# First modulation rows made in column strips beside the first norm, and the second norm's rows made between its tiles

## What is computed

```python
mod = jax.nn.silu(c) @ w_ada[l] + b_ada[l]            # [1, 6*1024]; w_ada is 1024 x 6144, f32
sh_m, sc_m, gt_m, sh_f, sc_f, gt_f = jnp.split(mod, 6, axis=-1)
h = modulate(rmsnorm(x, g_norm_mix[l]), sh_m, sc_m)    # h * (1 + sc) + sh
z = h @ w_in[l]                                        # r, k, v and low-rank columns, latent attention columns, gates
... RWKV-7 time mixing, latent attention ...
x = x + gt_m * ((sigmoid(gates) * branches) @ w_out)
h = modulate(rmsnorm(x, g_norm_ffn[l]), sh_f, sc_f)
x = x + gt_f * hierarchical_moe(h)
```

## Time and profile before

| | before |
|---|---|
| median of 3 runs | 1671.89 us (1671.5 to 1673.9) |
| profiled execution, its own time | 1669.98 us |
| its span | 1668.2 us |
| PE busy | 1427.4 us, 86% of the span |
| DVE busy | 704.3 us, 42% |
| ACT busy | 464.2 us, 28% |
| POOL busy | 249.0 us, 15% |
| mean granted TensorE clock | 0.923 of full |
| HBM read and written | 211.00 MB and 44.58 MB |

### The profile page before, as it was taken

One profiled execution on the slowest core, in us unless ns is written; L12 is line 12 of the kernel. 1 busy time (PEld: TensorE's weight loads), 2 busy tenths in 40 slices (PEclk: granted clock), 3 DMA queues, 4 the chain that ended last, 5 costly groups with the idle time before them and its releaser, 6 DMA issues. The chain is left out here.

```text
span 1668.2 us, 32819 instructions
## 1 busy us (share of the span) xinstructions
PE 1427.4 (86%) x14321; PEld 1024.3 (61%) x14321; DVE 704.3 (42%) x991; ACT 464.2 (28%) x827; POOL 249.0 (15%) x292
## 2 busy tenths in 40 slices
PE   7499999847999984499988999999896699999980
PEld 3497777627999981277767888787785333333320
DVE  1545677566666636144444111355335221111114
ACT  0543223252434322144434222212111111111110
POOL 0001122105656520011110000000000100000003
PEclk9699999978999997699998999999997699999995
DMA  6711222100000009990002111314106789999957
GB/s 256 251 56 51 83 81 83 58 15 2 5 4 4 4 8 318 313 371 1 1 1 76 50 50 50 139 51 152 42 39 260 265 326 420 421 421 401 410 212 302
DMA packets 76582, 252.35 MB, mean 151 GB/s; under 512 B 7128, under 2 KB 32216, under 8 KB 59680
## 3 DMA queue, kind: packets, MB, share of 16 engines
q1 hardware_dynamic: 66800, 220.48, 35.4%
q0 software_dynamic: 6048, 16.79, 2.8%
q10 hardware_dynamic: 3600, 13.11, 1.9%
HBM read 211.00 MB, written 44.58 MB: 153 GB/s over the span
## 5 line engine op out<-in xcount | busy, mean ns | idle before, releaser
L2418 PE MATMUL ps<-gu,xT 128*32 128x512 f32 x1536 | 178.3, 606 | 4.6 <-DMA gu<-w_e_up 3.9
L394 PE MATMUL ps<-hs,wh 128*128 128x512 f32 x320 | 126.7, 396 | 11.5 <-DVE hs L390 7.9
L396 PE MATMUL ps<-hs,wl 128*128 128x512 f32 x320 | 126.5, 395 | 0.0
L2418 PEld LDWEIGHTS ps<-gu,xT 128*32 128x32 f32 x1536 | 48.2, 112 | 111.6 <-issue 107.6
L2640 DVE TENSOR_TENSOR sg<-sg,ps 128x256 f32<-128x256 f32 x25 | 10.5, 422 | 217.3 <-ACT sg L2504 217.3
L395 PE MATMUL ps<-hs,wh 128*128 128x512 f32 x256 | 100.6, 393 | 0.0
L390 DVE TENSOR_TENSOR wl<-wraw,wh 128x1024 fp32r<-128x1024 f32 x24 | 29.4, 1225 | 156.2 <-ACT wh L387 156.2
L394 PE MATMUL ps<-hh,wr_h 128*128 128x512 f32 x224 | 93.1, 416 | 0.6 <-DVE wr_l L390 0.6
L395 PE MATMUL ps<-hl,wr_h 128*128 128x512 f32 x224 | 88.4, 395 | 0.0
L396 PE MATMUL ps<-hh,wr_l 128*128 128x512 f32 x224 | 88.4, 395 | 0.0
L1895 DVE TENSOR_REDUCE nmax<-ps 128x1 f32<-128x896 f32 (+4 forms) x64 | 45.9, 754 | 99.9 <-PE ps L1804 99.4
(11 more groups left out here) (358 smaller groups left out, 3037.0 us busy)
## 6 DMA issues: line engine op xcount, KB each, us to landing
gu<-w_e_gate SPq DMA_DIRECT2D x34, 1024.0 KB, 13.8
gu<-w_e_up SPq DMA_DIRECT2D x34, 1024.0 KB, 16.3
dn<-w_e_down SPq DMA_DIRECT2D x34, 1024.0 KB, 12.6
wada<-w_ada SPq DMA_DIRECT2D x16, 1024.0 KB, 6.7
expert_rows<-YTM ACTq DMA_DIRECT2D x25, 512.0 KB, 8.8
wbuf<-w_ada SPq DMA_DIRECT2D x4, 2048.0 KB, 15.5
wraw<-w_gates SPq DMA_DIRECT2D x16, 512.0 KB, 3.4
expert_rows<-zrow SPq DMA_DIRECT2D x4, 2048.0 KB, 24.6
```

The costliest lines, as they stand in the source:

```text
L394: nc.tensor.matmul(out, wt[0], mov[0], start=(k == 0), stop=False)
L396: return nc.tensor.matmul(out, wt[1], mov[0], start=False, stop=(k == kn - 1))
L2418: last = nc.tensor.matmul(ps[part, GB[b]], xT[:, b, k, part], gu[:, expert(m, c_) % WB, :, k], start=(k == 0), stop=(k == KD - 1))
```

## The change

Phase 0 is gone. Rows 0 and 1 are made at the start of phase 1 by `rows0`, with the strips of `Rows`: 8 pieces of 1 MB, each with its own slot. The result lies in four strips of one tile; four matmuls with a selection matrix `sel` as weights copy each strip to 128 partitions in PSUM, and ACT and DVE copy it to `SH_M` and `SC_M`. `rows4` moves from phase 4 into phase 1: 16 pieces of 256 columns (0.5 MB) with 3 slots, two pieces on PE after the transposes of each tile. The subtraction that gives `wm_l` moves from DVE to GpSimd. In phase 4 only `rows2` is left, with 6 slots, one piece per tile; pair 0 is loaded ahead of it, pairs 1 to 3 behind it and ahead of the stores of the results.

```diff
 class Rows:
-            def __init__(self, st, col, bank, row, other=None):
+            def __init__(self, st, col, bank, row, wbuf, crep, rep_s):
+                self.room, self.width = wbuf.shape[1], wbuf.shape[3]
+                self.pieces = KD * 512 // self.width
...
+            def load(self, sp, i):
+                if i >= self.room:
+                    sp.wait_ge(self.mm, i - self.room + 1)
+                at = slice(i // KD * self.width, (i // KD + 1) * self.width)
+                src = w_ada_v[:, i % KD, self.col:self.col + 2 * D].rearrange("p (j n) -> p j n", j=CH)[:, :, at]
+                sp.dma_start(self.wbuf[:, i % self.room], src).then_inc(self.w_in[i % self.room], 16)
...
-        with phase() as st:
...
-                    for b in range(CH):
-                        pe.wait_ge(w_in_s[b], 16)
-                        for k in range(KD):
-                            m = nc.tensor.matmul(ps[:, b], crep[:, k], wbuf[:, b, k],
-                                                 start=(k == 0), stop=(k == KD - 1))
...
 @block.sync
+                    sp.dma_start(ccol[:], c[0].rearrange("(p k) -> p k", k=KD)).then_inc(c_in, 16)
+                    sp.dma_start(cst[:], consts).then_inc(const_in, 16)
+                    rows0.load_bias(sp)
...
+                    for k in range(KD):
+                        rows0.load(sp, k)
+                        if k % 2:
+                            load_x(k // 2)
+                    sp.dma_start(wm[:], w_mla).then_inc(wm_in, 16)
+                    rows4.load_bias(sp)
...
+                    for i in range(NW):
+                        rows4.load(sp, i)
...
                     for t in range(NT):
+                        if t + 4 < NT:
+                            sp.wait_ge(h_ready, t + 1)
+                            load_x(t + 4)
+                        for i in range(NW + 2 * t, min(NW + 2 * t + 2, rows4.pieces)):
+                            rows4.load(sp, i)
+                        if t:
+                            store(t - 1)
+                    store(NT - 1)
+                    rows4.store(sp, 2)
 @block.gpsimd
+                    pool.wait_ge(wm_hi, 1)
+                    nc.gpsimd.tensor_tensor(wm_l[:], wm[:], wm_h[:].bitcast(f32), ALU.subtract).then_inc(wm_lo, 1)
 @block.scalar
+                    act.wait_ge(bc_mm, 1)
+                    nc.scalar.activation(SH_M, ps[:, 0:2].rearrange("p a n -> p (a n)"), ACT.Copy).then_inc(sh_ev, 1)
 @block.vector
+                    roots(0)
+                    rows0.add_bias(dve, CH + 2)
+                    dve.wait_ge(rows0.done, 1)
+                    nc.vector.scalar_tensor_tensor(row0[64:P], row0[64:P], 1.0, gains[64:P], ALU.add, ALU.mult)\
+                      .then_inc(rows0.done, 1)
+                    dve.wait_ge(bc_mm, 1)
+                    link(nc.vector.tensor_copy(SC_M, ps[:, 2:4].rearrange("p a n -> p (a n)")))
...
-                                low_part(wm_l[:], wm[:], wm_h[:]).then_inc(wm_lo, 1)
...
+                    rows4.add_bias(dve, CH + 2)
 @block.tensor
+                    for k in range(KD):
+                        rows0.products(pe, k)
+                    pe.wait_ge(rows0.done, 2)
+                    for j in range(CH):
+                        m = nc.tensor.matmul(ps[:, j], sel[:, j], row0, start=True, stop=True)
...
+                        for i in range(2 * t, 2 * t + 2):
+                            rows4.products(pe, i)
                         if t >= 2:
                             mla(t - 2)
 # phase 4, sync
+                    pair(0)
                     for k in range(KD):
                         rows2.load(sp, k)
-                    pair(0)
-                    for k in range(KD):
-                        rows4.load(sp, k)
-                    rows2.store(sp, 1)
+                    for p in range(1, HEADS // 2):
+                        pair(p)
                     for half in range(2):
                         sp.wait_ge(fin, NT * (half + 1))
...
-                    rows4.store(sp, 2)
-                    for p in range(1, HEADS // 2):
-                        pair(p)
+                    rows2.store(sp, 1)
 # phase 4, tensor
-                    for i in range(EARLY):
-                        row_products(i)
...
+                        rows2.products(pe, t)
```

More of the change, by code:

```diff
@@ L418, in build @@
             rot = alias("rot", [P, 2, 2, QK, 16], f32)
-            with ExitStack() as scratch:
-                ang = sb(scratch, "ang", [P, NT, 16])
-                turns = sb(scratch, "turns", [P, NT, 16])
+            arows = alias("arows", [P, 3, 512], f32)
+            row0, row4, gains = (arows[:, i] for i in range(3))
             sqk = sb(st, "sqk", [P, QK, QKD])
+            c_in, c_sig, rep_s, const_in, pc_in, sel_s, bc_mm, sh_ev = sems(
+                st, "c_in", "c_sig", "arep", "const_in", "pc_in", "sel_s", "bc_mm", "sh_ev")
+            rows0 = Rows(st, 0, 6, row0, wbuf0, crep, rep_s)
+            rows4 = Rows(st, 4 * D, 7, row4, wbuf4, crep, rep_s)
             x_in = slots(st, "x_in", 4)
@@ new lines, in _ @@
+                    for k in range(KD):
[4 more added lines that the diff above has]
+                    rows4.load_bias(sp)
+                    for j in range(2):
+                        half = slice(j * 512, (j + 1) * 512)
+                        sp.dma_start(gains[QUARTERS[j]], g_norm_ffn[:, half].broadcast_to([32, 512]))\
+                          .then_inc(rows4.b_in, 16)
@@ new lines, in _ @@
+                    for i in range(NW):
+                        rows4.load(sp, i)
+                    for b in range(2):
+                        sp.dma_start(wr[:, b], w_rwkv[b]).then_inc(wr_in[b], 16)
+                    sp.dma_start(pc[:], pcol).then_inc(pc_in, 16)
+                    sp.dma_start(posi[:], pos).then_inc(m_in, 16)
+                    sp.dma_start(g_row[:].rearrange("p a n -> p (a n)"),
+                                 qk_gain.broadcast_to([P, 2 * QKD])).then_inc(m_in, 16)
@@ L650, in tile_low, with roots @@
                         low_part(hl[:, :, cols], stage[:, t % 2], hh[:, :, cols]).then_inc(h_lo, 1)
-                    for half in range(2):
+                    def roots(half):
                         cols = slice(4 * half, 4 * half + 4)
@@ L670, in _ @@
                         tile_low(4 * half + 3)
+                    rows4.add_bias(dve, CH + 2)
+                    dve.wait_ge(rows4.done, 1)
+                    nc.vector.scalar_tensor_tensor(row4[0:64], row4[0:64], 1.0, gains[0:64], ALU.add, ALU.mult)\
+                      .then_inc(rows4.done, 1)
                     for b in range(2):
@@ L1595, in _ @@
                     rows2.load_bias(sp)
-                    rows4.load_bias(sp)
-                    for j in range(2):
-                        sp.dma_start(gffn[QUARTERS[j]], g_norm_ffn[:, j * 512:(j + 1) * 512].broadcast_to([32, 512]))\
-                          .then_inc(rows4.b_in, 16)
                     def pair(p):
```

145 lines of the change are left out of this document (50 added, 95 removed).

## The result

| | before | changed |
|---|---|---|
| median | 1672.33 us (1671.5 to 1673.9, 4 runs) | 1655.19 us (1648.97 to 1657.26, 4 runs) |
| profiled execution, its own time | 1669.98 us | 1648.97 us |
| its span | 1668.2 us | 1647.2 us |

The ratio is 0.989, 95% interval 0.9863 to 0.9918: faster by 17 us, inside the stated range of 1635 to 1657, but 8.7 us short of the forecast of 1646.5, outside the forecast's own 1640 to 1652 and only 1.8 us from the 1657 of rival 2.

The account below looks back on a forecast made before the run. TensorE idles at both changed places: the start, bound by DMA after the change, and the end of phase 4, bound by SP's loads and stores. +2.1 - 27.5 = -25.4 us gives 1644.6 profiled, 1646.5 median; range 1635 to 1657.

Parts of the forecast that it names:

- rival 2: Weights' DMA time was already hidden: stores wait for the drained queue (-19), phase 1 loses 4; 1657 us, chance 0.14.
- The likeliest case: The forecast itself: +2.1 us in phase 1, -27.5 in phase 4, 1646.5 us, own range 1640 to 1652, chance 0.66.
- What bounds the kernel: Both changed places have TensorE idle; strips save 22 us of TensorE time, but DMA takes over and keeps most.
- First scaling: Start of phase 1: first tile starts at 46.2 us instead of 52.88, 6.7 us sooner.
- the stream: Start of phase 1: 10.5 MB at 387 GB/s from 7.5 us, so the fourth tile of x lands at 34.6.
- The subtraction on GpSimd: Phase 1: wm_l takes 11.5 us on GpSimd, DVE operations beside it 2.8; 3 us of the 6.7 lead are left.
- The two ends differ by what DVE does: GpSimd's 2.5 to 3.7 ns a column depends on DVE's load; beside GpSimd, DVE operations take 2.76 and 2.87 us, not 1.28.
- The pieces of rows4 and the clock: Phase 1: pieces add 4.2 us over tiles 4 to 7, fuller clock gives back 0.8, semaphores net +1.6.
- Phase 4: Last result at 666.6, 15 us sooner; phase 6 starts at 677.8 instead of 705.34, 27.5 us sooner.
- I put the two stores there, 674.3: End of phase 4: stores go out at 674.3, last load at about 668, by the earlier held transfer's 5.2 us.
- The other end of the prediction: End of phase 4: stores wait until the nine loads drain (6.3 MB at 241 GB/s); phase 6 at 686 (-19).
- Rival 3: Phase 1: three half-size rows4 slots make PE wait if landing exceeds 9.7 us; at 17 us, 1679; chance 0.04.

Follow-up runs that it names:

- wm_l_in_four: Changed kernel, but GpSimd makes wm_l in four subtractions of 832 columns instead of one of 3328; 1648.62 us, ratio 0.9858 to the kernel before.
- old_order: Changed kernel, but in phase 4 the loads of pairs 1 to 3 are issued behind the stores, as before the change; 1650.22 us, ratio 0.9882 to before.
- stores_by_act: Changed kernel, but ScalarE issues the two stores of yT and the four of rows instead of SP; 1642.69 us, ratio 0.982 to before.
- after_again: The changed kernel run and profiled once more, with no edit; 1657.34 us, ratio 0.9899 to the kernel before.
- pairs_in_attention: Changed kernel, but the nine loads of pairs 1 to 3 are issued at the start of phase 6; 1641.75 us, ratio 0.9817 to before.
- wm_l_in_the_gap: Changed kernel, but ScalarE makes wm_h early and VectorE makes wm_l in idle time before copying SC_M; 1650.23 us, ratio 0.9874 to before.
- before_wm_l_on_pool: Kernel before the change, with only the wm_l subtraction moved to GpSimd behind g_row; 1675.2 us, ratio 1.0019 to before.
- more_semaphores: Changed kernel with 25 more, unused semaphores in the phase of the first norm; 1654.39 us, ratio 0.9901 to the kernel before.

## Why the prediction was right or wrong

The time lies in the stated range, but not in the narrower one that the forecast gave itself a chance of 0.66 for. The likeliest case was ahead of its rivals for the start but not for the end of phase 4: there the size is the one that rival 2 named.

**What bounds the kernel** was right: both places were idle places of TensorE, and the TensorE time that the strips save shows up nowhere, since DMA carries the start (each piece of `rows0` is waited for, up to 31.55). The saving is 15 us (29.37 against 14.4), not the 22 of the prediction; its own 1 to 1.9 us for each of eight pieces gives 14 to 21. The sum does not use this number.

**First scaling** was forecast at 46.2 and came at 44.01. The term that was mis-sized is the stream: 387 GB/s was what phase 0 moved with its four transfers of 2 MB, and the same queue moved 425 with pieces of 1 MB and tiles of x. The fourth square came at 32.80 instead of 34.6. The copying matmuls took 5.54 us, forecast 5.8. `g_row` was forecast to begin at 47.0 and began at 46.84.

**The subtraction on GpSimd** was forecast 11.5 us long with VectorE's operations at 2.8. It took 7.96 us, of which 7.1 were its own, and one VectorE instruction took 7.78. The step that failed is "The two ends differ by what DVE does". In the earlier trace rows two GpSimd operations of 768 columns meet VectorE operations, and all come out longer (2.76 and 2.87 us for 1.28, 2.78 for 1.90); I read that as a slowing of both. wm_l_in_four shows what it is: turns by whole instructions. For instructions of like length turns and slowing look much the same; for one long one they do not. The earlier trace rows had the same thing the other way round, unread: `g_row`, 96 columns, took 3.50 us beside VectorE's wm_l of 3.62, and takes 0.46 where it meets nothing. I took this 3.50 as the operation's own length. The Trainium skill (GPSIMD Engine Reference, section 8, Key points) has the contention, and that VectorE is about twice as fast elementwise. The traces agree with both: 7.1 to 7.2 against 3.62 us for the 3328 columns, and 7.78 for 1.22 us beside GpSimd.

The sum of this step came out all the same: three operations slowed by 4.6 us in all, or one stopped by 6.6. Tile 2's transposes were forecast at about 60.3 (51.3 and 8.4 make 59.7) and came at 59.69, the latent products at 63.8 and 63.46, tile 4 at 78.5 and 76.77. In the bad case tile 4 comes at 79.84. So the right number for the wrong reason, which is luck: the total that VectorE loses is near the same by both. The reason matters, because it decides which instruction stands still and so what waits for it, and by that it makes a part of the spread.

**The pieces of rows4 and the clock.** From tile 4's transposes to phase 2 it was 254.1 us and is 258.9: +4.8, where the terms (4.2 for pieces, -0.8 for the clock, +1.6 for semaphores) have +5.0. Each term was off, and they cancel. The pieces are 1.2 us a tile (6.61 for 5.41), not 1.06, so 4.8 for four tiles. The step from tile 4 to tile 5 had 1.62 us over the steady pace before (7.03 for 5.41) and has 0.04 now (6.65 for 6.61): the transposes of tile 4 take 1.09 us instead of 1.97, so TensorE is near its full clock there, and 1.6 us come back and not 0.8. The stretch of the semaphores is 1.63 longer, forecast 1.8 for these 25.

**Phase 4.** The last result was forecast 42.8 us into the phase and came at 42.4. SP's last load of the nine was forecast at 44.2 and came at 47.1. Then the step that failed: "I put the two stores there, 674.3", by the row of the transfer that had stood behind the nine loads. The stores went out at 682.4. The row was the nearest but not the same case: at the earlier trace rows the nine loads met an empty queue, here one that had been kept full since 653. The row was also misread: of the 5.2 us, 2.4 are the barrier (702.91 to 705.34) and only 2.80 the held issue, and 668 and 5.2 make 673.2, not 674.3. What the runs showed in its place is 10.25 us of issue for two stores, begun at 672.1.

The other end of the prediction, two stores that wait until the loads have drained, gave phase 6 at 686, and it started at 685.99. That they agree to this degree is luck. From the phase's own start it is 62.2 against 61.0, and the stores did not wait for the drain: SP had issued the second at 682.38, and the last load landed at about 688 (16.4 us behind its issue at 671.56).

Counted from the phase's own start, 54.0 us were forecast and 61.0 measured. Against the 1644.6 us forecast for a profiled execution the measured one is 4.4 longer: 7.0 of phase 4 and 1.1 of the phases between, less 2.0 at phase 2's start and 1.7 at the end. The other 4.3 us of the 8.7 are the difference between this execution and the median.

That the time of the loads was hidden by what followed is what rival 2 said. old_order bears it out for the move of the pairs (60.6 us, in the middle of what the new order takes), and stores_by_act shows the place to be SP's queue. The other half of rival 2, that phase 1 loses 4 us, did not come: phase 2 starts 0.15 us later.

**The sum against the medians.** The profiled execution was -21.0 us, the medians -17.1. A part of the difference is the start: two of the six profiles with that subtraction stand 4.4 us later there. How often the runs without a profile fall so is not known, and in after_again the start was less than half of the 10 us. The changed kernels in which no long GpSimd instruction meets VectorE spread over 3.6 to 5.8 us, the changed kernel in its two sets over 8 and 11. But old_order and pairs_in_attention, which have the long instruction, spread over only 4 in five runs, so this account rests on the profiles more than on the spreads, and that the start makes the spread of the times is not shown.

**Rival 3** did not come, as the landing times said, but it is not far: 1.44 us of waiting in the changed kernel, 5.0 in wm_l_in_the_gap. Its time at a landing of 17 us is 1680.6 by its own terms, not 1679.

What stays open: the stretches with unchanged code, from phase 2 to phase 4 and from phase 7 on, each differ by 4 to 5 us from profile to profile, and phase 4 with the new order by 4.0; I have no cause for it. Nor was it measured how much SP's queue holds. More slots for `rows4` were not tried.

## What to carry to other kernels

In these runs, where the instructions of both engines read two inputs from SBUF, work moved to GpSimd beside a busy VectorE takes nearly its own length from VectorE (6.6 to 6.9 us for 7.1), and which VectorE instruction stands behind it decides what waits. Put it where VectorE is idle. Cutting it into pieces shares the loss over several instructions and does not make it smaller (6.7 us over four); it helps when one instruction that others wait for would have had to bear all of it. Loads that are issued early for a later phase take the room in their engine's queue, and the short store behind them pays; issue what ends a phase from another engine's queue, or the loads behind the barrier. When a removed wait exposes a queue, price it by a row in which that queue was as full.

## What the runs showed of the hardware

- A VectorE instruction (1024 columns, both inputs in SBUF, 1.22 us alone) that begins while GpSimd runs a subtraction of 3328 columns ends 1.07 to 1.09 us after GpSimd's, and is 7.78 to 8.16 us long (the changed kernel, after_again, before_wm_l_on_pool, more_semaphores). It holds the other way too: 3.50 us for 0.46 on GpSimd, and the subtraction ends 7.1 us after the VectorE instruction that ran when it began (7.10 in the changed kernel, 7.08 in after_again). ScalarE's copies beside them kept their 0.60 us.
- With four GpSimd instructions of a quarter the size, the engines alternate: 2.61 to 2.93 us each on one, 2.85 to 2.97 on the other, of which 1.80 and 1.08 are their own turns.
- Behind nine loads SP's two stores took 10.25 us to issue (9.47 in after_again). With the same loads in SP's queue at the same place, ScalarE's queue took the same stores in 0.62 and 0.52 us (stores_by_act).
- Clearing a semaphore at a phase's end costs 0.064 us (1.59 for 25).
